# A decoder step whose opening is rebuilt: norm and turn of x beside the loading of the modulation weights, modulation made by feature, projection begun in feature groups

## What is computed

```python
mod = jnp.dot(jax.nn.silu(c), w_ada) + b_ada        # c: 1 row for the prompt, 8 for the samples
sh_a, sc_a, g_a, sh_f, sc_f, g_f = split(mod, 6)    # 1024 features each
z = _rms(x) * (1 + sc_a) + sh_a                     # _rms: x * rsqrt(mean(x * x) + EPS)
p = jnp.dot(z, w_in)                                # 1024 features in, 3072 columns out
```

## Time and profile before

| | |
|---|---|
| median of 3 runs | 1948.59 us (1942.55 to 1955.06) |
| the profiled execution's own time | 1950.54 us |
| its span in the profile | 1948.7 us |
| PE busy | 1705.4 us, 88% |
| DVE, ACT, POOL busy | 846.9, 540.9, 567.6 us |
| mean granted PE clock over the span | 0.931 of full |

### The profile page before, as it was taken

How to read it: one execution, slowest core, us unless ns; L and a number is a source line. 1 busy time by engine, 2 the same in 40 slices (tenths; PEclk the granted TensorE clock), 3 DMA queues, 4 the chain that set the end, 5 groups by cost and what they waited for, 6 DMA issues and landing times. The chain is left out here.

```text
span 1948.7 us, 22386 instructions
## 1 busy us (share of the span) xinstructions
PE 1705.4 (88%) x8256; PEld 1379.8 (71%) x8256; DVE 846.9 (43%) x1589; ACT 540.9 (28%) x784; POOL 567.6 (29%) x273
## 2 busy tenths in 40 slices
PE   6599999969999588876689689999999999999984
PEld 1488888857777476655568568887878787878863
DVE  3931222025555345564656313333333333333489
ACT  0322222225555145541225321111111111111121
POOL 0333323244000025584100132222222222222355
PEclk9699999989999688986789899999999999999997
DMA  7534443361210567764053211111111111111122
GB/s 269 190 135 149 174 152 130 109 196 42 60 32 0 161 191 216 223 205 145 2 171 105 76 44 44 44 43 43 43 43 43 43 43 43 43 43 43 43 86 92
DMA packets 136429, 192.95 MB, mean 99 GB/s; under 512 B 9643, under 2 KB 84443, under 8 KB 136228
## 3 DMA queue, kind: packets, MB, share of 16 engines
q1 hardware_dynamic: 124246, 169.68, 27.6%
q10 hardware_dynamic: 12128, 22.55, 3.1%
HBM read 163.20 MB, written 29.00 MB: 99 GB/s over the span
## 5 line engine op out<-in xcount | busy, mean ns | idle before, releaser
L2237 POOL TENSOR_TENSOR mlp_w_lo<-w_room,mlp_w_hi 128x2048 fp32r<-128x2048 f32 x31 | 143.5, 4631 | 320.5 <-ACT mlp_w_hi L2233 320.4
L2538 PE MATMUL ps<-mix_hi,mlp_w_hi 128*128 128x512 f32 x512 | 205.5, 401 | 15.2 <-DVE mlp_w_lo L2237 9.7
L2436 DVE TENSOR_TENSOR x<-x,ps 128x512 f32<-128x512 f32 x224 | 153.9, 687 | 142.3 <-PE ps L2609 141.5
L2415 DVE TENSOR_TENSOR mlp_h_lo<-mlp_pos,mlp_h_hi 128x512 fp32r<-128x512 f32 x64 | 69.4, 1084 | 333.0 <-ACT mlp_h_hi L2339 331.0
L2538 PE MATMUL ps<-mix_lo,mlp_w_hi 128*128 128x512 f32 x512 | 203.7, 398 | 0.0
L2538 PE MATMUL ps<-mix_hi,mlp_w_lo 128*128 128x512 f32 x512 | 203.6, 398 | 0.0
L2609 PE MATMUL ps<-mlp_w_hi,mlp_h_hi 128*128 128x512 f32 x448 | 175.9, 393 | 5.6 <-PE ps L2544 4.7
L2609 PE MATMUL ps<-mlp_w_hi,mlp_h_lo 128*128 128x512 f32 x448 | 174.5, 389 | 0.0
L2609 PE MATMUL ps<-mlp_w_lo,mlp_h_hi 128*128 128x512 f32 x448 | 174.3, 389 | 0.0
L603 POOL TENSOR_TENSOR inp_a_lo<-inp_room,inp_a_hi 128x2048 fp32r<-128x2048 f32 x24 | 110.5, 4605 | 215.8 <-ACT inp_a_hi L649 215.8
L628 PE MATMUL ps<-inp_whi,z_hi 128*128 128x512 f32 x384 | 151.3, 394 | 10.6 <-DVE inp_wlo L575 7.8
(11 more groups left out here) (361 smaller groups left out, 3444.7 us busy)
## 6 DMA issues: line engine op xcount, KB each, us to landing
w_room<-in_w_ff SPq DMA_DIRECT2D x32, 1024.0 KB, 7.0
inp_room<-in_w_ada SPq DMA_DIRECT2D x16, 1024.0 KB
proj<-inp_row ACTq DMA_DIRECT2D x54, 256.0 KB, 2.4
x<-in_cache_k SPq DMA_DIRECT2D x48, 256.0 KB, 5.3
cache_V<-in_cache_v SPq DMA_DIRECT2D x48, 256.0 KB, 4.5
mod_w<-in_w_ada SPq DMA_DIRECT2D x4, 2048.0 KB, 15.8
x<-in_x_prompt SPq DMA_DIRECT2D x16, 512.0 KB, 9.7
inp_room<-in_w_ada_f SPq DMA_DIRECT2D x8, 1024.0 KB
```

The costliest lines, as they stand in the source:

```text
L2237: pool.tensor_tensor(lo, raw, hi.bitcast(F32), ALU.subtract).then_inc(ready, 1)
L2415: dve.tensor_tensor(h_lo[s][:, j, cols], pos[u % 2][:], h_hi[s][:, j, cols].bitcast(F32), ALU.subtract).then_inc(h_ready, 1)
L2436: dve.tensor_tensor(dst, dst, ps[:, 5 + o % 3, :], ALU.add).then_inc(added, 1)
L2538: mm = pe.matmul(ps[:, u, :], w[:, k, j * P:(j + 1) * P], z[:, k, rows], start=(k == 0 and a == 0), stop=(k == KT - 1 and a == 2))
```

## The change

stage_modulation and norm_part are gone; all is one stage without a barrier or a way through DRAM for the two vectors.

- SP's queue loads x first, then the modulation weights in 4 blocks in the order (SH_A, SC_A) of features 0 to 511, (SH_A, SC_A) of 512 to 1023. They land in rooms that the projection uses later (`twins`: the same bytes under an fp32 name).
- The rows of x are summed (DVE and ACT share them), scaled and turned in two halves. Turned rows are copied to `full` without scale and shift.
- A modulation block is made by feature: 128 x 128 weights stand in the array and 9 columns of cT stream (L605 of the changed kernel), 32 products a block, results in PSUM by feature.
- Scale and shift are applied per feature group k over all 1024 rows (`features`), then `high_part` on ACT and `low_part` on DVE. The first chunk's weights are rounded by ACT (`first_high`) and subtracted by DVE (`first_low`).
- PE begins the first chunk with `early(k)`: the three products of group k for the six outputs that have a bank, 18 products. early(0) stands between the second and the third modulation block, early(1) to early(3) behind the fourth. In the first chunk outputs 0 to 5 then have only groups 4 to 7 left. The pieces keep their places after outputs 1, 3, 5 and 7.
- The first two chunks are written out; the loop has the other four.

```diff
+        MODS = [(m, h) for h in range(2) for m in (SH_A, SC_A)]
+        HALF = KT // 2
...
+        SUMS = [slice(0, TT // 2), slice(TT // 2, TT + 1)]
+        ada_room = [twins["whi1"], twins["wlo1"], room[:].rearrange("p (k c) -> p k c", c=CH)]
+
+        def ada_block(n, j):
+            if n < 3:
+                return ada_room[n][:, :, j * P:(j + 1) * P]
+            return twins[("a_hi", "a_lo")[j // 2]][:, :, (j % 2) * P:(j % 2 + 1) * P]
+
...
+
+            def modulation(n):
+                m, h = MODS[n]
+                col = m * D + h * CH
+                if n < 3:
+                    sp.dma_start(ada_room[n], ada[:, :, col:col + CH]).then_inc(ada_in[n], 16)
+                else:
+                    for j, name in enumerate(("a_hi", "a_lo")):
+                        sp.dma_start(twins[name],
+                                     ada[:, :, col + j * AW_CH:col + (j + 1) * AW_CH]).then_inc(ada_in[n], 16)
+
...
+            for t in range(TT):
+                sp.dma_start(x[:, t, :], io["x_prompt"][0, t * P:(t + 1) * P, :]).then_inc(x_in[t], 16)
+            sp.dma_start(xs, io["x_sample"].rearrange("b t d -> (b t) d")).then_inc(x_in[TT], 16)
+            modulation(0)
+            modulation(1)
             sp.sem_inc(raw_free, 2 * QUARTERS)
-            wait_all(sp, half_read)
-            load_weights(sp, 0, 0)
-            wait_all(sp, x_read)
+            sp.wait_ge(turned, KT)
+            first_weights(0)
+            first_weights(1)
+            modulation(2)
+            modulation(3)
+            first_weights(2)
+            first_weights(3)
+            sp.wait_ge(turned, 2 * KT)
             load_weights(sp, 0, 1)
-            wait_all(sp, z_ready)
+            sp.wait_ge(zs_turned, 1)
+            sp.wait_ge(mods_made, 3)
...
+            dve.memset(ss[:], 1.0).then_inc(cleared, 1)
+            dve.wait_ge(cleared, 2)
+            condition()
+            squares(0, 0)
+            squares(2, 1)
+            inverse_roots(0)
+            scale(0)
+            scale(2)
+            squares(4, 2)
+            squares(6, 3)
+            squares(TT, 4)
+            inverse_roots(1)
+            scale(4)
+            scale(6)
+            dve.tensor_scalar(xs, xs, rr[0:NS, TT:TT + 1], None, ALU.mult).then_inc(xs_done, 1)
+            for u in range(0, 2 * KT, 2):
+                take_turned(u)
+            take_mods(0)
+            take_mods(1)
+            features(0)
+            features(1)
+            first_low(0)
+            low_part(0)
+            features(2)
+            low_part(1)
+            features(3)
+            first_low(1)
+            low_part(2)
+            low_part(3)
+            take_mods(2)
+            take_mods(3)
+            features(4)
+            features(5)
+            low_part(4)
+            features(6)
+            low_part(5)
+            features(7)
+            sample()
+            low_part(6)
+            low_part(7)
+            dve.wait_ge(zs_hi, 1)
+            dve.tensor_tensor(zs[:, :, NS:P], smp_at, zs[:, :, 0:NS].bitcast(F32), ALU.subtract).then_inc(zs_done, 1)
+            first_low(2)
+            first_low(3)
             dve.sem_inc(added, 2)
-            split(0, 0)
             with dve.Fori(0, NCH // 2 - 1) as i:
                 split(i, 1)
                 pieces(i, 0)
@@ -597,6 +563,8 @@
 
         @block.gpsimd
...
+            def turn_rows(u):
+                h, k = divmod(u, KT)
+                if k == 0:
+                    pe.wait_ge(xn_dve, 2 * h + 2)
+                    pe.wait_ge(xn_act, 2 * h + 2)
+                if u >= BANKS:
+                    pe.wait_ge((ev_dve, ev_act)[u % 2], (u - BANKS) // 2 + 1)
+                for j in range(TT // 2):
+                    mm = pe.transpose(ps[:, u % BANKS, j * P:(j + 1) * P], x[:, 4 * h + j, k * P:(k + 1) * P], ident[:])
+                mm.then_inc(turned, 1)
+
+            def modulation(n):
+                m, h = MODS[n]
+                pe.wait_ge(ada_in[n], 16 if n < 3 else 32)
+                if n == 2:
+                    pe.wait_ge(mods_done, 2)
+                for j in range(HALF):
+                    for k in range(KT):
+                        mm = pe.matmul(mods_made_at[:, m, h * HALF + j, :], ada_block(n, j)[:, k, :], cT[:, k, :],
+                                       start=(k == 0), stop=(k == KT - 1))
+                mm.then_inc(mods_made, 1)
...
+
+            def early(k):
+                pe.wait_ge(z_done, k + 1)
+                weights_split(0, 0, k // (KT // QUARTERS))
+                for o in range(BANKS):
+                    products(ps[:, o, :], o, 0, [k])
+
+            def chunk(i, s, first=False):
+                for o in range(OUTS):
+                    n = s * OUTS + o
+                    bank = ps[:, n % BANKS, :]
+                    pe.wait_ge(bank_free, i * 2 * OUTS + n + 1)
+                    if first and o == 0:
+                        pe.wait_ge(z_done, KT)
+                    if first and o == TT:
+                        pe.wait_ge(zs_done, 1)
+                    half_done = first and o < BANKS
+                    for k in range(HALF if half_done else 0, KT):
+                        if o == 0 and k % (KT // QUARTERS) == 0:
+                            weights_split(i, s, k // (KT // QUARTERS))
+                        mm = products(bank, o, s, [k])
+                    mm.then_inc(made, 1)
+                    if o % 2 and o < TT:
+                        piece(i, s, o // 2)
+                pe.wait_ge(made, i * 2 * OUTS + (s + 1) * OUTS)
+                pe.sem_inc(w_free, 1)
+
+            turn_small()
+            for u in range(2 * KT):
+                turn_rows(u)
+            pe.wait_ge(c_ready, 1)
+            modulation(0)
+            modulation(1)
+            pe.wait_ge(xs_done, 1)
+            for k in range(KT):
+                mm = pe.transpose(smp_at[:, k, :], xs[:, k * P:(k + 1) * P], ident[0:NS, 0:NS])
+            mm.then_inc(zs_turned, 1)
+            pe.wait_ge(ev_dve, KT)
+            pe.wait_ge(ev_act, KT)
+            early(0)
+            modulation(2)
+            modulation(3)
+            for k in range(1, HALF):
+                early(k)
+            chunk(0, 0, first=True)
+            chunk(0, 1)
+            with pe.Fori(1, NCH // 2) as i:
                 for s in range(2):
...
-                    pe.sem_inc(w_free, 1)
+                    chunk(i, s)
...
+            for u in range(1, 2 * KT, 2):
+                take_turned(u)
+            act.wait_ge(sums_act, 4)
+            first_high(0)
+            high_part(0)
+            high_part(1)
+            first_high(1)
+            high_part(2)
+            high_part(3)
+            high_part(4)
+            high_part(5)
+            high_part(6)
+            high_part(7)
+            act.wait_ge(zs_full, 1)
+            act.copy(zs[:, :, 0:NS], smp_at).then_inc(zs_hi, 1)
+            first_high(2)
+            first_high(3)
+            act.wait_ge(mods_made, len(MODS))
+            act.wait_ge(zs_done, 1)
             act.sem_inc(bank_free, BANKS)
...
-            stage_modulation(nc, io, ps, ident, mod_p, x, xs[0:NS, :], ss, c_parts)
+            twins = unrounded_twins(nc)
             z_hi, z_lo, zs = feature_parts(c, "z")
-            heads = stage_projection(nc, io, ps, ident, mod_p, z_hi, z_lo, zs, x, xs, ss, c_parts)
+            heads = stage_projection(nc, io, ps, ident, twins, z_hi, z_lo, zs, x, xs, ss, c_parts)
```

More of the change, by code:

```diff
@@ new lines, in first_low, with sample @@
+            def first_low(q):
+                k = quarter(q)
+                dve.wait_ge(w_hi_done, q + 1)
+                dve.tensor_tensor(w_lo[0][:, k, :], raw[0][:, k, :], w_hi[0][:, k, :].bitcast(F32),
+                                  ALU.subtract).then_inc(raw_free, 1)
+            def sample():
+                steps = Steps(dve, s_steps)
+                by_seq = smp_at.rearrange("p k (b t) -> p k b t", t=DS)
+                for m, op in ((SC_A, ALU.mult), (SH_A, ALU.add)):
+                    for h in range(2):
+                        ks = slice(h * HALF, (h + 1) * HALF)
+                        dve.wait_ge(zs_turned, 1)
+                        steps.then(dve.tensor_tensor(by_seq[:, ks], by_seq[:, ks],
+                                                     mods[:, m, ks, 1:NC].unsqueeze(3).broadcast_to([P, HALF, DB, DS]), op))
+                dve.sem_inc(zs_full, 1)
@@ new lines, in parts_of, with products @@
+            def parts_of(o, s):
+                if o < TT:
+                    return slice(o * P, (o + 1) * P), ((z_hi, w_hi[s]), (z_hi, w_lo[s]), (z_lo, w_hi[s]))
+                return slice(0, P), ((zs, w_hi[s]), (zs, w_lo[s]))
+            def products(bank, o, s, ks):
+                cols, parts = parts_of(o, s)
+                for k in ks:
+                    for a, (z, w) in enumerate(parts):
+                        mm = pe.matmul(bank, z[:, k, cols], w[:, k, :], start=(k == 0 and a == 0),
```

(13 more changed lines are left out.)

359 lines of the change are left out of this document (136 added, 223 removed).

## The result

The changed kernel takes 1962.35 us (median of 10 runs, 1956.63 to 1974.97) and the kernel before, beside it, 1947.84 (10 runs): ratio **1.0077, 95% interval 1.0052 to 1.0101**. It is slower by 10 to 20 us, 0.5 to 1.0%. The forecast was 1962.5.

A forecast was written before the change was run, and what follows sets the result against it. PE was taken to bound the kernel; four stretches put the fourth piece at 148.4 us against 134.51, 13.9 later, so 1962.5 us from the median of 1948.6. Range for 8 in 10: 1941 to 1974.

The forecast's parts named there:

- the mark: Start of the fourth piece on PE: 148.4 us against 134.51, 13.9 later; behind it both kernels do the same.
- Turning: First stretch, x loaded, scaled and turned on PE: ends at 31.5 us.
- The modulation: Second stretch, 256 records on PE: clock lost after 3.4 us, 25.0 us a pair of blocks, 50.0 against 29.6 before.
- 256 r - 36.1: Change in us, r being the mean us of a modulation record: nil at r = 0.141, 1% slower at 0.217.
- The early products: Third stretch: first group starts at 61.0 after 4.5 us of DVE and takes 6.1; the other 54 products take 14.3.
- T: End of the second pair of modulation blocks on PE, forecast at 92.1 us.
- The first chunk: Fourth stretch: PE stalls 1.6 and 6.1 us for pieces, so the fourth piece starts at T + 56.3.
- the chain of 20.5 us: From the first piece's end until POOL is done on the third; taken to be no faster after the change.
- Pieces don't stall, clock lost: Rival, first chunk: no stalls, 7.7 + 1.5 us less, 4.7 slower, 1953 us; chance 0.07.
- Clock kept: Rival, modulation blocks: clock stays up, 0.11 us a record, 8 us faster, 1941 us; chance 0.15.
- Cold throughout: Rival: turning does not lift the clock, blocks cost 28.5 us a pair, 24 slower, 1972.6 us; chance 0.14.
- no overlap: Rival, modulation: loads and streams don't overlap, 0.34 us a record, 51 slower, 2000 us; chance 0.05.

The follow-up runs named there:

- experiment 2: Changed kernel with DVE's two additions of the first piece ahead of the last quarter of the second chunk's split: 1957.64 us, 1.0049 of the kernel before.
- experiment 6: Changed kernel with the first feature group's early products moved behind the fourth modulation block: 1954.84 us, ratio 1.0022 to the kernel before.
- experiment 5: Changed kernel with the third and fourth modulation blocks mixed with the products begun early: 1975.63 us, ratio 1.0136 to the kernel before.
- the last kernel of experiment 8: Changed kernel, modulation still by feature, with pieces moved and all early products behind the fourth block: ratio 0.9992 to the kernel before.
- experiment 4: Changed kernel with 14, 30 or 62 needless wide products in the first two modulation blocks: ratios 1.0105 and 1.0109, with 62 1.0109, to the kernel before.
- experiment 1: Changed kernel with the pieces of the first two chunks moved behind other outputs: 1952.28 us, ratio 1.0022 to the kernel before.

## Why the prediction came out

**The mechanism was right, and the mark came 4.8 us earlier than forecast (143.6 for 148.4). That the time was met to 0.2 us is luck: behind the mark as much came on top, which no step had foreseen.**

*Turning* ended at 29.4, not 31.5. I took 0.22 us a block, but the clock was already rising (0.86 from 26 to 30), so that the last 40 took 6.1 us. DVE's first copy came at 22.6 for 23.5. The rise, from 0.50 at 26 to 1.00 at 28, came before any wide product or block, as at 64.0: it came while PE did nothing but turn x, in both kernels.

*The modulation* is the term that was mis-sized. The mechanism was right: 0.11 us a record, then 0.213 ((79.14 - 72.31) / 32) with the clock at 0.50. The warm start was 4.5 and 4.9 us where I took 3.4, so that 41 and 44 records ran warm and not 31, and a cold record took 0.213 for my 0.2225: 45.9 us against 50.0, or r = 0.179 against 0.195. By the formula 256 r - 36.1 that is +9.8; turning (2.1 earlier) and the first chunk (1.3 later) make it the measured 9.05.

*The early products* took 6.2 us for 6.1, behind a DVE chain of 4.5 for 4.5. T was 86.0 instead of 92.1: 2.1 from turning and 4.1 from the blocks.

*The first chunk* took 57.6 us from T for 56.3 (14 early products ran cold behind the fourth block, not 10), with waits of 1.55 and 5.83 us for 1.6 and 6.1, and ACT's rounding waited for a DMA as said. I read the chain of 20.5 us as a property of the piece's stream. With DVE's additions in time the third piece came 16.3 and 16.1 us behind the first one's end (experiments 2 and 6), for 20.5 in the change: 4.2 us of the chain are DVE's order and its addition of 4.35 us beside POOL, and with the third piece at the low clock (3.5 us for 1.8) they cost 6.1. The row with DVE's 4.76 us beside POOL's 4.61 was in my hands; I used its length and did not ask what order would avoid it.

*Behind the mark* I said that both timelines are alike. So the sum with the measured mark would have been 1948.6 + 9.05 = 1957.7, 4.7 us below the result, though the interval reaches down to +10. Against the kernel before as it ran beside (1947.84) it is 5.5, of which the traces show 1.9; the other 3.5 are that the profiled execution of the kernel before was 2.7 us above its median and that of the change 0.8 below. In the profiles the difference was 8.3 us at the first product of attention, 7.9 at 742 us, 11.8 at 873 and 10.95 from 1108 on. It grew in the cached attention, where the same stage met another clock:

```profile
800.00:820.00 20.00, 14.29 (x79) 11.54 (x78) 12.43 (x31) 10.79 (x15) 4.57 (x2) 0.91 0.68 208
```

```profile
809.00:829.00 20.00, 14.41 (x69) 11.83 (x69) 11.51 (x30) 9.73 (x14) 2.94 (x2) 0.75 0.66 196
```

The first is of before, the second of after. Whether the change causes this or it is chance isn't settled: the stage was not touched, and in the 14 profiles, all alike there, it took from the sample's heads to retention between 256.3 and 261.4 us. The kernel before took 258.4 and the change 261.4, but with experiments 5 and 6 and the last kernel of experiment 8 there are three more above 261, while the other slower ones (experiment 4) took 256.3 to 258.2.

*The rivals.* "Pieces don't stall, clock lost" was priced at 1953: experiment 1 made it and got 1952.28. "Clock kept" was priced at 8 us faster; no run kept it for nothing, but with half the products the two pairs took 26.6 us less and the mark came 26.6 earlier, so it goes with the blocks' time on PE. "Cold throughout" and "no overlap" fell by the rows of L605. That turning does not lift the clock, from which "cold throughout" has its 33 us, no run shows: in every one the clock was at 1.00 when turning ended.

## What to carry over

A product that loads 128 columns to stream 9 took 0.11 us a record here, and in a long stream the clock fell to 0.50 after 4.1 to 5.5 us, for itself (0.213 us a record) and for what followed. Try the small operand in the array and stream the large one, even if the result must then be turned: here it was 13.9 us a pair for 23.1. When work is brought forward so that PE's stretches between two dependent steps get shorter, go through each engine's queue and ask what stands ahead of the step that others wait for; here two additions of 0.41 us behind a split cost 6 us. And an early start in a gap was worth nothing, because it used up another engine's slack.

## What I had not expected of the hardware

- One wide product behind every second of those small ones kept the clock at 1.00 for 7.9 us of the pair instead of 4.5, and then it fell; one behind every product kept it there for all of its 25 us.
- A stretch that started cold and mixed both kinds (30 wide products, 128 small records) stayed at 0.50 for the 40 us shown, its wide products included.
- In a stage that is identical in all kernels, retention, the clock took different courses. The 24 us from 950 in the kernel before and their counterpart in experiment 2:

```profile
950.00:962.00 12.00, 10.81 (x57) 7.87 (x55) 6.12 (x26) 0.22 (x1) 6.46 (x2) 1.00 0.02 7
962.00:974.00 12.00, 3.84 (x18) 2.76 (x17) 8.14 (x31) 1.23 (x2) 0.00 (x0) 0.63 0.00 0
```

```profile
949.00:961.00 12.00, 10.82 (x34) 7.81 (x34) 2.97 (x6) 0.00 (x0) 5.01 (x2) 0.58 0.02 5
961.00:973.00 12.00, 11.65 (x36) 8.11 (x35) 6.51 (x28) 0.53 (x2) 0.00 (x0) 0.50 0.00 0
```

From the first row of retention (L1227) to the first output product it took 80.4 to 80.8 us in ten profiles, and 85.0 to 87.7 in four. So 4 to 7 us between two executions can be of this kind, which is why a mark in the trace tells more here than a few runs.
